# A hybrid decoder layer: GpSimd instead of VectorE makes the low parts of the weights in the joint phase

## What is computed

```python
h = rms_norm(x, norm_pre_mix);  proj = h @ w_in
q, k, v, qi, ki, wi, hq, hf, hi, hg = split_columns(proj)
q, k, qi, ki = partial_rope(...)                       # first 16 of 64 dims
att = dsa_attention(q, k, v, qi, ki, wi * idx_scale)   # 256 keys a query, by the indexer
hg  = hgrn2_mixer(hq, hf, hi, hg)
x = x + rms_norm(concat(att, hg) @ w_out) * norm_post_mix
h2 = rms_norm(x) * norm_pre_ffn
x = x + rms_norm((silu(h2 @ w_gate) * (h2 @ w_up)) @ w_down) * norm_post_ffn
```

## Time and profile before

| | |
|---|---|
| median of 3 runs | 3402.47 us (3401.07 to 3404.37) |
| the profiled execution, its time | 3398.05 us |
| its span, first to last instruction | 3396.3 us |
| granted TensorE clock, mean | 0.982 of 2.4 GHz |
| busy share of TensorE, VectorE, ScalarE, GpSimd | 95%, 66%, 44%, 7% |

### The profile page before, as it was taken

The page is one execution under the profiler, slowest core; times in us unless marked ns, Lnnn a source line. Parts: engine busy times, 40 slices in busy tenths (PEclk is TensorE's granted clock), DMA queues, the critical chain, the costliest instruction groups (busy, mean ns, idle before and its releaser), DMA issues.

```text
span 3396.3 us, 46669 instructions
## 1 busy us (share of the span) xinstructions
PE 3232.0 (95%) x18176; PEld 2852.3 (84%) x18176; DVE 2248.5 (66%) x3721; ACT 1499.6 (44%) x2477; POOL 227.1 (7%) x400
## 2 busy tenths in 40 slices
PE   8999999999888899999989999998999999989998
PEld 8999999999767688888778888887888888878886
DVE  3467677778555776666787677767876865463444
ACT  3454445455354544444455444445554444333222
POOL 0000000000110200010101001011000000010000
PEclk9999999999899999999999999999999999999999
DMA  5543443343221322222332222224211112252233
GB/s 182 167 127 126 131 146 108 128 141 129 97 85 68 111 74 83 78 86 72 139 122 71 71 75 74 66 89 164 70 67 62 55 61 72 90 186 96 90 104 108
DMA packets 147501, 345.75 MB, mean 102 GB/s; under 512 B 15056, under 2 KB 35920, under 8 KB 145232
## 3 DMA queue, kind: packets, MB, share of 16 engines
q1 hardware_dynamic: 144976, 338.55, 29.9%
q10 hardware_dynamic: 2304, 4.20, 0.3%
HBM read 283.38 MB, written 59.31 MB: 101 GB/s over the span
## 4 chain that ended last, share of the span: by engine, by line
PE 63%; DVE 5%; ACT 2%; issue 2%; DMA 1%; POOL 0%; DVEq 0%; SPq 0%; ACTq 0%; POOLq 0%
PE PJ_d L2040 9%; PE PJ_d L2042 9%; PE PJ_d L2041 9%; PE SC L2000 6%; PE PJ_d L2065 6%; PE PJ_d L2067 6%; PE PJ_d L2066 6%; PE SA L1959 4%; PE SA L1960 3%; PE SA L1986 3%; PE SA L1955 1%; DVE wd_lo L1800 1%; DVE prob L1785 1%; DVE h_lo L1805 1%; ACT h_hi L1566 0%
## 5 line engine op out<-in xcount | busy, mean ns | idle before, releaser
L2040 PE MATMUL PJ_d<-h_hi,wd_hi 128*128 128x512 f32 (+1 forms) x1472 | 577.6, 392 | 19.7 <-DVE h_lo L1805 17.7
L2042 PE MATMUL PJ_d<-h_hi,wd_lo 128*128 128x512 f32 (+1 forms) x1472 | 565.1, 384 | 0.0
L2041 PE MATMUL PJ_d<-h_lo,wd_hi 128*128 128x512 f32 (+1 forms) x1472 | 564.0, 383 | 0.0
L1556 ACT ACTIVATE wd_hi<-wd_raw 128x512 fp32r<-128x512 f32 x568 | 344.7, 627 | 232.1 <-DMA wd_raw<-in_w_gu 132.8
L720 PE MATMUL PJ<-w_hi,h_hi 128*128 128x338 f32 (+1 forms) x1280 | 416.3, 325 | 2.8 <-DVE w_lo L546 2.8
L1551 ACT ACTIVATE pT<-SA 128x512 f32<-128x512 f32 (+3 forms) x320 | 156.7, 532 | 587.7 <-PE SA L1986 587.7
L1800 DVE TENSOR_TENSOR wd_lo<-wd_raw,wd_hi 128x512 fp32r<-128x512 f32 x568 | 380.1, 688 | 50.3 <-ACT wd_hi L1556 47.3
L721 PE MATMUL PJ<-w_lo,h_hi 128*128 128x338 f32 (+1 forms) x1280 | 409.0, 320 | 0.0
L722 PE MATMUL PJ<-w_hi,h_lo 128*128 128x338 f32 (+1 forms) x1280 | 408.9, 319 | 0.0
L1785 DVE CUSTOM_DVE_ANT_0 prob<-SA,bias 128x1024 f32<-128x1024 f32 (+7 forms) x192 | 170.1, 911 | 319.9 <-PE SA L1960 312.6
L2040 PEld LDWEIGHTS PJ_d<-h_hi,wd_hi 128*128 128x128 f32 x1472 | 281.2, 191 | 70.5 <-DVE h_lo L1805 11.3
(11 more groups left out here) (202 smaller groups left out, 5737.9 us busy)
## 6 DMA issues: line engine op xcount, KB each, us to landing
wd_raw<-in_w_gu SPq DMA_DIRECT2D x352, 256.0 KB, 2.8
wd_raw<-in_w_down SPq DMA_DIRECT2D x176, 256.0 KB, 2.6
w_raw<-in_w_in SPq DMA_DIRECT2D x40, 684.0 KB, 4.6
w_raw<-in_w_in SPq DMA_DIRECT2D x40, 676.0 KB, 4.5
row_h<-proj_d SPq DMA_DIRECT2D x16, 1024.0 KB, 7.1
proj_d<-stage SPq DMA_DIRECT2D x40, 342.0 KB, 4.3
proj_d<-stage SPq DMA_DIRECT2D x40, 338.0 KB, 5.1
x_d<-acc SPq DMA_DIRECT2D x24, 512.0 KB, 2.6
```

The lines of the kernel that those rows point to most:

```text
L1556: s_.activation(w_hi[:, u % RING, :], w_raw[:, u % RING, :], ACT.Copy).then_inc(w_hi_ready, 1)
L2040: t.matmul(to[:, tok], w_hi[:, r, w], h_hi[:, c, tok], start=(c == 0 and part != 1), stop=False)
L2041: t.matmul(to[:, tok], w_hi[:, r, w], h_lo[:, c, tok], start=False, stop=False)
L2042: last = t.matmul(to[:, tok], w_lo[:, r, w], h_hi[:, c, tok], start=False, stop=(c == KD - 1 and part != 0))
```

## The change

GpSimd gets `split_unit` and does it in its own step n, the step in which ScalarE makes the high part; VectorE's `split_unit` in step n + 1 is gone. `prep(b + 2)` on GpSimd moves from the top of block b to behind the segments of head 0. The reduction at head 6 stays where it was.

```diff
@@ gpsimd @@
+            def split_unit(u):
+                pool.wait_ge(w_hi_ready, u + 1)
+                g.tensor_tensor(w_lo[:, u % RING, :], w_raw[:, u % RING, :], w_hi[:, u % RING, :].bitcast(F32), ALU.subtract)\
+                 .then_inc(w_lo_ready, 1)
+
             def step(n):
                 for what, back, ends in (("mix", 2, last_out), ("x1", 4, last_out), ("ff", 2, last_down)):
                     if ends(n - back):
                         s, i = item_at(n - back)[1], item_at(n - back)[4]
                         root(root_no(s, what, i))
+                for u in splits_at.get(n, []):
+                    split_unit(u)
...
             for b in range(NB):
-                if b + 2 < NB:
-                    prep(b + 2)
                 for c in range(pairs_of(b + 1) if 2 <= b + 1 < NB else 0):
                     for h in range(IH):
                         fill(("i", b, c, h))
                 fill(("s", b))
                 for h in range(HEADS):
+                    if h == 1 and b + 2 < NB:
+                        prep(b + 2)
@@ vector @@
-            def split_unit(u):
-                dve.wait_ge(w_hi_ready, u + 1)
-                v.tensor_tensor(w_lo[:, u % RING, :], w_raw[:, u % RING, :], w_hi[:, u % RING, :].bitcast(F32), ALU.subtract).then_inc(w_lo_ready, 1)
...
-                for u in splits_at.get(n - 1, []):
-                    split_unit(u)
```

## The result

The change makes the kernel slower: 3429.58 us in the median (3424.39 to 3433.45), against 3403.42 us for the kernel before beside it. The ratio is 1.0075, with an interval of 1.0056 to 1.0094, so some 26 us. The profiled execution has a span of 3431.7 us, 35.4 more than that of before: it was the slowest of the four of the changed kernel (3433.45 us), and the profiled one of before (3398.05 us) is faster than all four of its runs, so some 9 of the 35 us belong to this pair of executions and not to the change. A few single executions in later runs took 10 to 15 ms, with the kernel before as well; comparisons and ranges leave them out.

The account below looks back on a forecast made before the run. TensorE, busy 95% of the span, was taken as the bound, so VectorE's relief counts only in four seams. Sum: -12 - 6 + 15.5 + 3.5 = +1 us, forecast 3403 us, range 3384 to 3421.

Parts of the forecast that it names:

- the sum's seam term, -12 - 6: At the four starts of a group of four blocks (seams), VectorE's relief wins 12 us idle time and 6 us clock.
- 17.2 us off the chain: Low parts' total on the chain in three seams (100, 150, 80 us); two thirds, 12 us, were taken as gain.
- Rival 2: VectorE held by GpSimd's reads of the same memory, seams longer: 3445 us at most, 3425 more likely; chance 0.10.
- a mean cost of 0.17 us an operation: VectorE's average hold, from GpSimd's 28% occupancy and half of a 1.2 us subtraction.
- Rival 2's "half", 3425 us: Half of the extra in the 3445 us worst case of VectorE held by GpSimd, called more likely.
- the stalls: TensorE waits for late low parts behind the reduction at head 6 in five blocks: 15.5 us, plus 3.5 clock.
- The change of code ahead of the reduction: GpSimd's code load before the head 6 reduction: taken at 7.1 us, bounds 0 and 7.1.
- A subtraction on GpSimd: Each of the 568 moved subtractions of 128x512 takes 1.2 us on GpSimd, 680 us in all.
- The moved rotation: Rotation on GpSimd behind head 0: cost 0, up to 3 us among the root operations of a seam.
- Late nowhere by itself: GpSimd's 1.2 us subtractions, started a step sooner, are hidden by three or more steps of slack; cost nothing.
- VectorE's busy time should have fallen by 380 us: Over the whole kernel, VectorE loses 568 subtractions of 688 ns, 380 us of 2248; a sign of being right.
- the sign that had been set for rival 2: VectorE's operations with two SBUF operands clearly longer than before, or gaps ahead of them.

Follow-up runs that it names:

- run 2: The changed kernel, but VectorE makes the low parts at the four starts of a group of four blocks again (87 units): 3414.75 us, ratio 1.0037.
- run 5: The kernel before, but nobody makes low parts in the joint phase; the third product reads the high part again: 3394.08 us, ratio 0.9975.
- run 7: The changed kernel, but GpSimd copies left on each partition in place of the reduction over partitions: 3415.13 us, ratio 1.0039.
- the twin: The kernel before, rotation moved, plus one GpSimd subtraction of 128x448 from SBUF at each unit into a tile nobody reads: 3445.47 us, ratio 1.0126.
- fills: The kernel before, rotation moved, plus four GpSimd fills with zeros at each unit into a tile nobody reads: 3412.9 us, ratio 1.0031.
- run 1: The changed kernel, but VectorE takes back 65 low parts behind the reductions (head 6 segment C, openings, head 7 segments A, B): 3417.55 us, ratio 1.0049.
- run 10: The kernel before with only the rotation of the later block's rows moved behind head 0: ratio 1.0001.
- run 9: The changed kernel, but VectorE makes the low parts at group starts and behind the reductions, GpSimd the other 423: 3403.78 us, ratio 1.0003.
- run 12: The kernel before, with VectorE's own subtractions one step later at the starts of the groups: 3432.35 us, ratio 1.009.
- run 13: The kernel before without low parts, rotation moved, plus an unread GpSimd subtraction from SBUF at each unit: 3 us below its expected 3412 to 3418 us.

## Why the prediction was wrong

**The step that failed is the sum's seam term, -12 - 6.** It came out at about +20 in the trace and, by the medians of the change and run 2, at about +15. It failed twice.

- *Its size.* The relief is 8 us (run 5), clock included. Reading 17.2 us off the chain (in three of the four seams; the third, 2280 to 2400 us, has another 2.0 in the trace of before) and taking two thirds was too much: with the low parts gone, the waits of TensorE on h_lo in the largest form were still 14.2 us, against 17.7. Other work ended last at once.
- *The term that I left out.* Rival 2 was the mechanism, and I set it at 0.10 with a mean cost of 0.17 us an operation, from GpSimd's share of the time and half of a subtraction. In this kernel the mean for the two operations on hid was 255 and 328 ns (693 to 948, 431 to 759). A mean over an even spread was the wrong price. Of the 88 products into hid 23 were held (26%, about GpSimd's share), but each for 0.97 us and not for half of 1.2; of the 88 scalings 46 were held (52%), for 0.63 us each. Why they meet at these moments was not tested; a likely reason is that both engines are let go by the same products. I had the row for it, the copy of V that took 291 to 1326 ns. It showed GpSimd held, and I let that stand for the whole. Both were held: GpSimd's subtraction has a median of 1292 and a mean of 1384 ns, and the copy of one column in run 7 took 1330 ns in the mean.

Rival 2's "half", 3425 us, is 4.6 us off the result, and that is partly luck. As it was put, it turns the seams from 0.67 us an operation; that is what the four scalings in the fourth seam paid (1284 to 1964 ns), the other operations less. But the gain to be cancelled was 8 us, not 18, and the seam of 150 us has not 27 but at least 42 operations of 256 or more columns with two operands in SBUF in the trace of before. Of the Trainium skill, SBUF — State Buffer, section Who interferes with whom, three statements can be set beside rows: VectorE with two SBUF inputs contends with a GpSimd instruction that reads SBUF (688 to 920 ns with the twin), not with one that only writes (688 with fills), and with one SBUF input it does not (685 and 685). The Trainium skill excepts, in the same section, a faster mode of operations such as the scaling, which contends in any case: of the shapes with eight or more operations the fills lengthened by over 10 ns only three, all of the scaling's kind, hid's from 431 to 528 ns, one on score from 771 to 824 and one on 128x8 elements from 233 to 294. All of it agrees; by that rule rival 2 deserved a greater chance.

**The step that held is the stalls.** I worked out 3.5, 2.5, 3.6, 3.8 and 2.1 us, in blocks 3, 6, 9, 10 and 13. The waits of TensorE on GpSimd's wd_lo are 2.3, 2.1, 3.1, 2.7 and 3.5 us, at 1120, 1490, 1949, 2112 and 2651 us: 13.6 instead of 15.5. With their clock, run 7 puts them at 14.5 us and run 1 at 12, against 19 forecast. The change of code ahead of the reduction, bounded between 0 and 7.1 us and taken at 7.1, is 5.8 to 6.5 us in seven of the eight cases that show it, and 8.5 in block 13, whose stall came out 1.4 us longer than worked out; the one behind is 7.3. The Trainium skill, GPSIMD Engine Reference, section Instruction dispatch, has about 6 us for the first call of a freshly loaded kernel. Ahead of the reduction the trace agrees (6.5 us in the mean), behind it the price is more, and this case pays on both sides.

**The other steps.** A subtraction on GpSimd was taken at 1.2 us; its shortest is 1.25, its mean with the holding 1.38. The moved rotation costs nothing (run 10), as forecast. "Late nowhere by itself" holds in the steady stretches (run 9) but not in a seam: there TensorE waited 2.3 us at 3011 us for GpSimd's low part, and run 12 shows that a seam has no three steps of slack. VectorE's busy time should have fallen by 380 us and fell by 242, the sign that had been set for rival 2.

**The sum as measured.** 3402.5 - 8.5 (relief, run 5) + 14.5 (twin on top of it, run 13) + 14.5 (change of code, run 7) = 3423. The changed kernel is at 3429.6. The 6.6 us that are missing are no more than the intervals of these terms together. What may stand in them is queueing behind a subtraction that is longer than the twin (1.38 against 1.23 us), and the unit that came 2.3 us late; this was not settled. From the other side the account closes: 3429.6 - 12 - 14.8 = 3402.8, measured as 3403.8 (run 9).

No version that keeps the low parts beat the kernel before. The 8 us of relief would have to come from an engine that doesn't hold VectorE by its reads; no run tried one.

## What to carry to other kernels

Work moved from VectorE to GpSimd is not free because GpSimd is idle: if it reads SBUF, price each of VectorE's operations with two operands there that can meet it, on the critical stretch, at up to the length of GpSimd's instruction, and don't average over time. A fill in place of the moved operation, beside a twin that nobody waits for, tells holding from queueing in two runs, if both keep GpSimd busy for the same time. Before putting steady work on GpSimd behind an instruction that changes its code, look for the idle time that ends with nothing shown, and count it ahead of that instruction as well as behind.

## What the hardware showed that was not expected

- Both engines pay for a meeting: two subtractions on GpSimd took 3.50 us where pairs elsewhere take 2.50 to 2.53, and VectorE's scaling beside them 2.20 instead of 1.28 us.
- Even the smallest operations are caught: one of VectorE's on 128x2 elements went from 223 to 315 ns in the mean, and GpSimd's copy of 128x1 (run 7) took 449 to 2182 ns, until the VectorE operation under which it had begun was over.
- GpSimd's change of code costs nearly as much ahead of the reduction (6.5 us in the mean, 6.05 in block 10) as behind it (7.3 us); 36 us of waiting hid the first in the kernel before.
- The hold is all or nothing: the 23 products into hid that began while a GpSimd instruction ran were held, and no other was; with fills none of 62 was.
